# Attention group C in an encoder trunk: one score item per step two units ahead, negated scores, 128 value columns, two of four map mixes on GpSimd

## The reference

```python
logits = jnp.einsum('bqhid,bshid->bhiqs', qb, k).astype(f32) * scale      # i = 0, 1: two maps
bias = -slopes[:, None, None, None] * jnp.abs(qp[:, None] - pos[None, :])[None, None]
p = jax.nn.softmax(logits + bias, axis=-1)
a = (p[:, :, 0] - lam * p[:, :, 1]).astype(v.dtype)
return jnp.einsum('bhqs,bshe->bqhe', a, v)                               # v: 64 columns a head
```

## Time and profile before

| | us |
|---|---|
| median of 3 runs | 3109.83 (3108.21 to 3112.62) |
| profiled execution | 3105.02 |
| its span, first to last instruction | 3102.9 |
| busy in the span: PE / DVE / ACT / POOL | 2951.7 / 2085.3 / 1341.1 / 430.0 |
| units 7 / 8 to 14 / 15, layer 0 | 23.9 / 141.8 / 17.0 |

### The profile page before, as it was taken

How to read it: one execution, slowest core, us unless ns; L and a number is a source line. 1 busy time by engine, 2 the same in 40 slices (tenths; PEclk the granted TensorE clock), 3 DMA queues, 4 the chain that set the end, 5 groups by cost and what they waited for, 6 DMA issues and landing times.

```text
span 3102.9 us, 40020 instructions
## 1 busy us (share of the span) xinstructions
PE 2951.7 (95%) x13464; PEld 2295.2 (74%) x13464; DVE 2085.3 (67%) x2449; ACT 1341.1 (43%) x1835; POOL 430.0 (14%) x227
## 2 busy tenths in 40 slices
PE   6999889998999999999999997999999999999997
PEld 4777634886778888888877784368777888888885
DVE  5887887994265655556768789879725555565557
ACT  3226777993322221222323387779723222222224
POOL 3111211222300000000131022112232000000002
PEclk8999999999999999999999999999999999999998
DMA  4354322423111111111136632234211211112112
GB/s 181 144 172 122 70 60 61 96 61 102 48 55 41 55 54 41 54 41 41 38 129 206 171 80 53 52 82 91 91 56 45 64 41 54 41 45 63 41 41 65
DMA packets 236928, 236.51 MB, mean 76 GB/s; under 512 B 67632, under 2 KB 199664, under 8 KB 236784
## 3 DMA queue, kind: packets, MB, share of 16 engines
q1 hardware_dynamic: 236784, 234.71, 26.7%
HBM read 183.81 MB, written 50.86 MB: 76 GB/s over the span
## 4 chain that ended last, share of the span: by engine, by line
PE 73%; issue 13%; DVE 5%; POOL 4%; ACT 3%; DMA 1%; ACTq 0%; SPq 0%; DVEq 0%; POOLq 0%
PE ps L1637 28%; PE ps L1652 14%; PE ps L1490 8%; PE ps L1550 6%; PE ps L1400 5%; PE ps L1524 3%; PE ps L1528 3%; PE ps L1529 3%; PE ps L1622 2%; POOL w0l L630 1%; POOL prob L660 1%; ACT prob L839 1%; PE ps L1566 1%; DVE r L1120 1%; POOL rstd L619 1%
## 5 line engine op out<-in xcount | busy, mean ns | idle before, releaser
L1490 PE MATMUL ps<-stack 128*128 128x512 f32 (+1 forms) x1152 | 333.9, 409 | 46.7 <-ACT prob L839 46.3
L1318 DVE TENSOR_TENSOR xT<-ps,xT 128x512 f32<-128x512 f32 x352 | 241.1, 690 | 203.8 <-PE ps L1652 203.5
L839 ACT ACTIVATE prob<-ps,nmx 128x1024 f32<-128x1024 f32 x320 | 355.9, 1112 | 41.6 <-DVE nmx L1140 29.3
L1550 PEld LDWEIGHTS ps<-cst,prob 128*128 128x128 f32 x2048 | 245.5, 141 | 152.2 <-ACT ptf L900 45.4
L1550 PE MATMUL ps<-cst,prob 128*128 128x128 f32 x2048 | 315.9, 277 | 13.4 <-DVE ptl L1238 6.3
L630 POOL TENSOR_TENSOR w0l<-wraw,w0h 128x1024 fp32r<-128x1024 f32 x32 | 80.4, 2517 | 1601.3 <-ACT w0h L740 1601.3
L1490 PEld LDWEIGHTS ps<-stack 128*128 128x128 f32 (+1 forms) x1152 | 203.4, 189 | 121.4 <-ACT prob L839 67.4
L1238 DVE TENSOR_TENSOR ptl<-ps,pth 128x512 fp32r<-128x512 f32 x384 | 259.3, 685 | 42.1 <-ACT pth L900 38.1
L1283 DVE SCALAR_TENSOR_TENSOR cv<-u,vec,cv 128x1024 f32<-128x1024 f32 x176 | 225.9, 1283 | 90.8 <-ACT cv L975 80.4
L987 ACT ACTIVATE ah<-cv 128x1024 fp32r<-128x1024 f32 x44 | 46.7, 1061 | 537.0 <-DVE cv L1296 537.0
L1138 DVE TENSOR_REDUCE nmx<-ps 128x1 f32<-128x1024 f32 x192 | 234.0, 1219 | 63.3 <-PE ps L1490 61.6
(11 more groups left out here) (207 smaller groups left out, 5619.1 us busy)
## 6 DMA issues: line engine op xcount, KB each, us to landing
wraw<-in_w_up SPq DMA_DIRECT2D x88, 512.0 KB, 4.7
draw<-in_w_down SPq DMA_DIRECT2D x22, 1024.0 KB, 4.9
wraw<-in_w_in SPq DMA_DIRECT2D x33, 512.0 KB, 3.9
stack<-ka_d SPq DMA_DIRECT2D x64, 256.0 KB, 5.3
vst<-v_d SPq DMA_DIRECT2D x48, 256.0 KB, 3.9
x_d<-xT SPq DMA_DIRECT2D x2, 4096.0 KB, 18.1
wraw<-in_w_out SPq DMA_DIRECT2D x16, 512.0 KB, 6.1
stack<-qc_d SPq DMA_DIRECT2D x64, 128.0 KB, 3.5
```

The costliest lines, as they stand in the source:

```text
L839: act.activation(two(dst), score_banks(i), ACT.Exp, bias=nmx[:, b, i:i + 1], scale=scale, accum_out=rsum[:, b, i:i + 1]).then_inc(exp_done, 1)
L1318: ins = dve.tensor_tensor(xs, ps[:, 4 + j % 4, :], xs, ALU.add)
L1490: ins = pe.matmul(score_banks(i)[:, kh, :], st[q][0:rows, c0:c0 + P], st[k][0:rows, kh * HALF:(kh + 1) * HALF], start=n == 0, stop=n == le ...
L1550: ins = pe.transpose(ps[:, 4 + s % 2, m * P:(m + 1) * P], prob[:, b, m, s * P:(s + 1) * P], ident)
```

## The change

- Two items of a C unit are made two units ahead (`ahead` gives 2 for C, 1 for A and B from the third unit on), at steps 6 and 7, the other six at steps 0 to 5, one per step, always before the step's transposes. ACT takes each exponential one step later and ahead of that step's copy; item 0 of the unit after next waits for the transposes of the unit whose buffer it takes.
- The query scale constant is negated, DVE adds the distance, multiplies by the slope and reduces with min, so the reduction gives the negated maximum itself: L1140 and the wait before it go.
- Map 1 has four buffers (`prob1a`, `prob1b`), one per block.
- For blocks 0 and 1 DVE forms only the ratio; POOL scales map 1 (a new tensor_scalar) and adds. ACT's `scale_map` goes. DVE still mixes blocks 2 and 3.
- The value product loads the 128 columns of a pair of heads and writes all 128 PSUM rows; `vfull` doubles.
- ACT copies the norm of a C unit at step 7 and DVE takes the reciprocal of the sums at step 1.

```diff
-STEP_OF = {..., 8: {0: [0, 1], 1: [2], 2: [3], 3: [4], 4: [5], 5: [6, 7]}}
+STEP_OF = {..., 6: {0: 2, 1: 3, 2: 4, 3: 5, 4: 6, 5: 7}}
+EARLY_STEP_OF = {"A": {7: 0}, "B": {7: 0}, "C": {6: 0, 7: 1}}
+EXP_STEP_OF = {..., 6: {0: 1, 1: 2, 2: 3, 3: 4, 4: 5, 5: 6, 6: 7}}
+MIX_STEPS = {2: 0, 4: 1, 6: 2, 7: 3}
+POOL_MIXES = (0, 1)
...
-            return y["k"] >= 2 and "C" not in (y["group"], head((y["k"] - 1) // 2)[0])
+            return (2 if y["group"] == "C" else 1) if y["k"] >= 2 else 0
...
-                        sp.dma_start(vfull[hh % 2][:, :, :], ...[:, :, h * HD:(h + 1) * HD]).then_inc(full, 16)
+                        sp.dma_start(vfull[hh % 2][:, :, :], ...[:, :, h // 2 * P:(h // 2 + 1) * P]).then_inc(full, 16)
...
+                def mix_maps(x, q):
+                    b, n = x["half"], l * (2 * NC * NPM) + NPM * (x["u"] - U_C) + POOL_MIXES.index(q) + 1
+                    pool.wait_ge(ratio_done, n)
+                    settle(pool)
+                    pool.tensor_scalar(second_map(q), second_map(q), rinv[:, b, 2 * q + 1:2 * q + 2], None, ALU.mult).then_inc(map_scaled, 1)
                     pool.wait_ge(map_scaled, n)
+                    pool.tensor_tensor(prob[:, b, q, :], second_map(q), prob[:, b, q, :], ALU.add).then_inc(mixed_first, 1)
                     pool.wait_ge(mixed_first, n)
...
                 def pool_unit(x, prev, nx, after):
+                    if second:
+                        mix_maps(nx, POOL_MIXES[0])
                     if prev:
                         scale_output(prev)
+                    if second:
+                        for q in POOL_MIXES[1:]:
+                            mix_maps(nx, q)
+                    if prev:
                         lo_mix(prev)
...
+                        if i == 0:
+                            act.wait_ge(trans_done, l * (8 * NU) + (x["u"] - 1) * 8)
...
+                        if second and item is not None:
+                            exp_item(nx, item)
+                        if s == 7 and after and after["group"] == "C":
+                            exp_item(after, 0)
                         act.wait_ge(trans_done, l * (8 * NU) + x["u"] * 8 + s + 1)
...
-                        step(dve.tensor_tensor_reduce(src, src, two(dtab[:, off:off + T]), 1.0, -3.0e38, ALU.subtract, ALU.max, mx[:, b, i:i + 1]))
+                        dve.tensor_tensor_reduce(src, src, two(dtab[:, off:off + T]), SLOPES[x["h"]], 3.0e38, ALU.add, ALU.min,
+                                                 nmx[:, b, i:i + 1]).then_inc(max_done, 1)
-                    dve.tensor_scalar(nmx[:, b, i:i + 1], mx[:, b, i:i + 1], -scale, None, ALU.mult).then_inc(max_done, 1)
...
-                        pe.matmul(ps[part_rows(x)[0], 6 + b, :], vfull[x["par"]][:, s, :], ptf[:, s % NPT, :],
+                        pe.matmul(ps[:, 6 + b, :], vfull[x["par"]][:, s, :], ptf[:, s % NPT, :],
...
-            cst[p, C_SC + t] = SCALE_C / SLOPES[2 * t + p // HD]
+            cst[p, C_SC + t] = -SCALE_C / SLOPES[2 * t + p // HD]
```

More of the change, by code:

```diff
@@ L186, in build @@
         pth, ptl = sb(ph2, "pth", [P, NPT, HALF], F32R), sb(ph2, "ptl", [P, NPT, HALF], F32R)
[L187 removed]
+        prob1a = sb(ph2, "prob1a", [P, 2, T])
         vst1 = sb(ph2, "vst1", [P, TT, P], F32R)
@@ L889, in hi_mix @@
                     act.activation(mix_at(xgh, x), osum[rows, :], ACT.Copy).then_inc(mix_hi, 1)
-                def scale_map(x):
-                    act.wait_ge(ratio_done, l * (2 * NC) + x["u"] - U_C + 1)
-                    act.activation(prob1[:, 0, :], prob1[:, 0, :], ACT.Copy, scale=rinv[:, x["half"], 1:2]).then_inc(map_scaled, 1)
                 def act_unit(x, prev, nx, after):
                     for s in range(8):
+                        second = nx and nx["group"] == "C"
+                        item = EXP_STEP_OF[own_items(nx)].get(s) if nx else None
+                        if second and item is not None:
+                            exp_item(nx, item)
+                        if s == 7 and after and after["group"] == "C":
+                            exp_item(after, 0)
                         act.wait_ge(trans_done, l * (8 * NU) + x["u"] * 8 + s + 1)
@@ L900, in act_unit @@
                         act.activation((ptf if x["group"] == "C" else pth)[:, s % NPT, :], ps[:, 4 + s % 2, :], ACT.Copy).then_inc(pt_hi, 1)
-                        for i in EXP_STEP_OF[own_items(nx)].get(s, ()) if nx else ():
-                            exp_item(nx, i)
+                        if not second and item is not None:
+                            exp_item(nx, item)
                         if s == 3 and prev:
                             copy_part(prev)
-                        if s == 3 and nx and nx["group"] == "C":
-                            scale_map(nx)
                         if s == 7 and prev:
                             hi_mix(prev)
-                        if s == 6:
+                        if s == (7 if x["group"] == "C" else 6):
                             copy_norm(x)
@@ L1229, in dve_unit @@
                     for s in range(8):
[L1230 to L1233, removed]
+                        if nx and s in STEP_OF[own_items(nx)]:
+                            max_item(nx, STEP_OF[own_items(nx)][s])
+                        if after and s in EARLY_STEP_OF[after["group"]]:
+                            max_item(after, EARLY_STEP_OF[after["group"]][s])
                         if nx and nx["group"] == "C" and s in MIX_STEPS:
-                            mix_maps(nx, MIX_STEPS.index(s))
+                            mix_maps(nx, MIX_STEPS[s])
                         if x["group"] != "C":
@@ L1533, in pe_unit @@
                     for s in range(8):
[L1534 to L1537, removed]
[L1538 to L1540 removed]
+                        if nx and s in STEP_OF[own_items(nx)]:
+                            score_item(nx, STEP_OF[own_items(nx)][s])
+                        if after and s in EARLY_STEP_OF[after["group"]]:
+                            score_item(after, EARLY_STEP_OF[after["group"]][s])
                         if s == 0:
                             if x["group"] == "C":
[L1543 to L1544 removed]
+                                pe.wait_ge(mixed_first, l * (2 * NC * NPM) + NPM * (x["u"] - U_C + 1))
+                                pe.wait_ge(mixed, l * (2 * NC * NDM) + NDM * (x["u"] - U_C + 1))
                             else:
@@ L1551, in pe_unit @@
                         ins.then_inc(trans_done, 1)
-                        if not early:
-                            for i in items:
-                                score_item(nx, i)
                         if s >= LAG:
```

55 lines of the change are left out of this document (24 added, 31 removed).

## The result

| | before | changed |
|---|---|---|
| median | 3109.83 us | 3126.47 us (5 runs, 3123.55 to 3127.24) |
| profiled span | 3102.9 us | 3125.1 us |

The ratio is 1.0054, with a 95% interval of 1.0040 to 1.0068: slower by half a per cent, where 3072 us was forecast. The ratios of the experiments are to the kernel before as it ran beside them (median 3108.83 us).

What follows compares the result with a forecast made beforehand. DVE was taken as the bound in C units. Units 8 to 14 -14.4, 7 -1.9, 6 +1.6, 15 -3.1, 16 -0.8 gave -18.6 a layer, -37.2 in all: 3105.0 to 3067.8, plus 4.8 to the median, 3072; range 3045 to 3100.

Steps and rivals of the forecast that it cites:

- one stretch a layer at 1.3 us: TensorE in units 8 to 14: one half-clock stretch left in each layer's sum, costing 1.3 us.
- each unit gets one: Clock rival: the longer gap brings every C unit a half-clock stretch, 6 more a layer at 1.3 us, 3088; chance 0.06.
- the gap (2.6 us: TensorE idles once, some 2.6 us before step 0 of each C unit, until DVE's last mix ends.
- The scaling on POOL: POOL's new tensor_scalar on map 1 of blocks 0 and 1: 1.2 us each, bounds 1.15 to 2.37.
- The longhand schedule: Step-by-step times of one C unit on TensorE, DVE and POOL, ending between 17.7 and 18.8 us.
- Four such instructions a unit: POOL would run four instructions a C unit that DVE's two-SBUF-input operations wait for, instead of one.
- DVE's item: DVE's work on one C score item, falling from 1.48 to 1.32 us without the scaling by -slope.
- the TensorE step: Scores, transposes and 128-column product on TensorE: 1.77 us a step, 0.28 less than before.
- Unit 15: Unit without a C unit to prepare: 3.1 us less, from one moved A item and eight shorter TensorE steps.
- The longhand unit of 18.2 us: Duration taken for a middle C unit, against 20.1 before, with DVE as the bound.
- The slower rival: POOL's scaling over 2.4 us makes DVE wait, paid twice a unit; at 3.5 us the whole is 3125; chance 0.08.
- signs of being wrong: POOL's scaling outside 1.15 to 2.37 us, no gap before the unit, or clocks falling in most units.

Runs made afterwards that it cites:

- warm: The changed kernel with 24 identity transposes on TensorE before it waits for DVE's last mix of a C unit; 3091.48 us, 0.9942 of before.
- before_neg: The kernel before with only the negated scores added (min instead of max, slope inside the reduction); 3099.34 us, 0.9971.
- warm_ratio: The changed kernel with 24 filling transposes before the wait for DVE's last mix and the one-tensor-input ratio; 3065.64 us, 0.9856.
- ratio_ts: The changed kernel with DVE's small ratio as tensor_scalar, one tensor input and two per-partition scalars; 3082.73 us, 0.9917.
- act_scale2: The changed kernel with ACT instead of POOL scaling map 1 of blocks 0 and 1, POOL only adding; 3117.09 us, 1.0025.

## Why the prediction was wrong

The direction was wrong. Two steps of it failed on the costly side, one on the other.

What it said of the clock rests on layer 0, where one of units 8 to 14 had a stretch at half clock. Layer 1 of the same trace, said to repeat it closely, has three, in units 8, 10 and 13 (columns as in the earlier trace rows):

```profile
1886.10:1906.70 20.60, 17.60 (x68) 9.35 (x68) 18.73 (x39) 16.37 (x28) 5.04 (x3) 0.93 0.29 67
...
1926.70:1948.00 21.30, 19.34 (x69) 8.30 (x70) 17.71 (x38) 15.60 (x27) 3.81 (x3) 0.92 0.33 75
...
1988.00:2009.40 21.40, 19.33 (x69) 8.29 (x69) 17.80 (x38) 15.55 (x27) 3.91 (x3) 0.92 0.13 28
```

- **Half clock: this is the larger error.** The prediction had one stretch a layer at 1.3 us and gave "each unit gets one" 0.06. It also forecast the gap (2.6 us, seen 3.2 and more) ahead of every unit. The runs show that this gap brings a stretch in every unit, at 2.2 us each in the mean of units 8 to 13: 34 us in both layers (`warm` against the changed kernel). The 0.06 rested on "one unit in seven had it", and with layer 1 it was four in fourteen. Before, the idle 1.43 us came with other idle around it; that was read as a small risk, when the forecast itself had doubled the idle in one piece.
- **DVE's waits for POOL were under-counted.** The scaling on POOL was taken as 1.2 us with 2.37 as the upper bound. It takes 2.85, outside both ends, and is slower than POOL's two-input addition. The half-for-half-the-inputs reasoning was wrong, and so was the estimate of 0.88 us worked out from the Trainium skill (GPSIMD Engine Reference, section 3.1). The longhand schedule had ratio 1 waiting for next to nothing (9.21 + 0.45 = 9.66, POOL's addition ending at 9.62); it waits 1.6 because POOL's addition ends 1.65 us later. The last ratio and the last product lose 0.8 and 1.1, where one loss of about 1.1 was feared and half of it counted. Making the ratios one-input took off 28 us in both layers with the filler in, 3.2 of them clock in unit 15; the products' waits are still there.
- **Which of POOL's instructions hold DVE** was read too widely. "Four such instructions a unit" counts both scalings, and the row behind it shows only an addition. The two additions and L662 hold DVE's two-input instructions; the scaling holds none (30 of 32 at their free length).
- **DVE's item was over-priced**, 1.32 for 1.14 (`before_neg`): 8 x 0.18 = 1.4 us a unit in the other direction.
- **Held:** the TensorE step, 1.76 us from product to product in `warm` for a forecast 1.77, and unit 16 at 12.5 for 12.8. Unit 7 went to 21.6 (22.0 forecast). Unit 6 grew by 2.7 instead of 1.6: TensorE idles 0.88 us before the second early item too, which the prediction did not see, beside 0.83 before the third.
- **Unit 15** was put at 13.9 and took 16.7 in the changed kernel, 14.6 in `warm_ratio` without half clock: the price of its own work was right within 0.7, the rest is clock.
- The longhand unit of 18.2 us is what `warm_ratio` shows (18.2 in the mean of units 8 to 14). That is luck: errors cancel in it. POOL's scaling is longer than assumed, DVE's items are shorter, and the ratio in that kernel doesn't wait at all.
- The **rivals** named the mechanisms, each with its own small chance: exclusion with a scaling over 2.4 us (3125, chance 0.08) and the clock (3088, 0.06). What came is both at once, linked: the exclusion lengthens the gap, and the gap costs the clock. They were added up as if only one could happen, and the range stopped at 3100, short of both together. The slower rival's 3125 is near the measured 3126 for half the wrong reason: at nearly full clock the same kernel with all its exclusion takes 3091, less than before. Of the prediction's signs of being wrong two came, POOL's scaling outside 1.15 to 2.37 and the clock fallen in most units.

## What to carry to other kernels

Before work is moved to POOL, look through DVE's instructions for two SBUF inputs, however small: beside a two-input instruction of POOL each one begun beside it lasted at least until that one ended. POOL's one-input scaling did not hold them; it hurt by its length (2.85 us). A one-column ratio with one tensor input and per-partition scalars was worth 44 us of 3126, part of it through the clock (28 with the gap filled). It was worth nothing in the kernel before, where a two-input product stood right behind it. When a change gathers TensorE's idle into one piece, price the clock behind it, and try filling the piece with idle transposes before anything else is redesigned.

## Of the hardware, not expected

- POOL's tensor_scalar of 128x1024 f32 with a per-partition scalar takes 2.85 us, its tensor_tensor of the same size 2.37.
- In the changed kernel gaps of 3.2 to 4.9 us came with half clock (0.5, 1.2 GHz) in all 16 C units. Where gaps were 2.1 to 2.5 us (`ratio_ts`, units 10 to 14) 5 of 10 units had it, and with 12 filling transposes units 8 to 14 had none. A gap of 3.0 us ahead of unit 15 in `act_scale2` had none behind it, and units 11 and 13 of `before_neg` had a stretch with no gap ahead of them. The granted clock stayed at 0.5 for 3.4 or 6.8 us each time.
- Beside POOL's addition (tensor_tensor, two inputs) all 32 one-column ratios of the changed kernel that began there ended within 0.03 us of its end. Beside POOL's scaling (tensor_scalar, one input) 30 of 32 two-input instructions of DVE had their free length, the other two 0.2 us more.
- A one-column scalar_tensor_tensor on DVE with two SBUF inputs lasted up to 2.23 us, a one-column tensor_scalar 0.27 in all 64 cases.
- The f32 product pair with 64 columns goes at 1.00 us and with 128 columns at 0.86, and the transposes behind it start without the extra wait that the earlier trace rows show.
